# A mixture-of-experts layer on one core: where TensorE's code behind the expert loop begins within a fetch block

## The chip, the cores and the metric

The kernel runs on one core of a Trainium2 chip. The metric is the device time of one execution in microseconds (us), the median of three runs. Beside the times there is one profiled execution, whose trace holds every instruction of the engines (PE for TensorE, DVE for VectorE, ACT for ScalarE, POOL for GpSimd, SP for SyncE) and every DMA packet, among them the packets by which the engines fetch their own instructions.

## The reference

One decoder layer with 256 tokens and a model width of 2048: token mixers (attention and a gated branch), a norm, and then a mixture of 16 experts, which is where the change lies. Each token goes to two experts of one group of four.

```python
def grouped_moe(h, router_w, router_b, w_gate, w_up, w_down):
    ...
    aff = jax.nn.softmax(logits, axis=-1)
    ...
    best_group = jnp.argmax(group_score, axis=-1)
    ...
    top_val, top_idx = lax.top_k(masked, TOP_K)
    top_w = top_val / top_val.sum(-1, keepdims=True)
    combine = jnp.sum(jax.nn.one_hot(top_idx, N_EXPERTS, dtype=jnp.float32) * top_w[..., None], axis=1)
    ...
    for e in range(N_EXPERTS):
        hid = jax.nn.silu(t @ w_gate[e]) * (t @ w_up[e])
        y = y + combine[:, e:e + 1] * (hid @ w_down[e])
    return y.reshape(B, S, D)
...
    f = grouped_moe(hm, router_w, router_b, exp_w_gate[l], exp_w_up[l], exp_w_down[l])
    x = layer_norm(DEEPNORM_ALPHA * x + g2 * f, ln2_g[l], ln2_b[l])
```

Everything is float32. One expert has 2048 x 1024 weights for gate, for up and for down.

## The kernel before, in words

SP queues the weights in order as 2 MB loads into a ring of buffers in SBUF; a load waits until PE has used the buffer that it overwrites (L713). From about 778 us on, the weights of the 16 experts are streamed, and PE, DVE and ACT run through the experts in step. PE gathers an expert's tokens into slots, multiplies them with gate and up, turns the result, multiplies with down, and scatters the rows back by matmuls (`add_up`, L941, which waits for DVE).

The code of an expert depends on the number of its tokens, which is known only when the kernel runs. `CLASSES` (L43) names the cases: up to 32 tokens (`few`), up to 64 (`wide`), and then `one_extra`, `two_extra` and `all_extra` with further sets of slots. The code for `few` stands in the loop `pe_experts` itself. For every expert PE loads the count (L1665) and asks once whether it is above 32 (`ask_once`, L821). If it is, PE jumps out of the loop, to code that stands behind the whole loop and behind the kernel's last part. That code is built by `begin_and_go_on` (L830): a part `more`, which asks for the class (L835) and holds the beginning of each class (`begin`) and a jump to the body (L842); and the body of each class with the rest of the expert, a semaphore's increment (L846) and a return to the loop (`leave`, L853). The jump's target can be announced by a hint: L1219 in the `few` code for the jump of the next expert, L840 for the jump to the body, L1253 for the return.

With the tokens of this data four experts are above 32: the third of the first group (107 tokens, `two_extra`), the third and the fourth of the second group (65, `one_extra`, and 51, `wide`) and the first of the last group (90, `one_extra`). The bodies have 2173, 1293, 539 and 1293 instructions.

The loop's start is set in this way already, to slot 100 (`LOOP_SLOT`, L1657). Behind the loop stands `pe_experts_end` with the last norm's matmuls (L1673 to L1685, helper line L1280), which ends with the jump to the program's end (L279), and behind that the `more` parts and bodies of all 16 experts, four bodies each.

Of the kernel before, what the change touches and what calls it, by code (L numbers as in the profile page):

```python
# [275 lines left out]
def program(nc, x_tok_d, x_T_d, c_T_d, rel_bias_d, router_w_d, router_b_d, ada_w_d, ada_b_d, ada_bT_d, w_in_d,  # L276
            sgu_g_d, sgu_b_d, sgu_wT_d, sgu_bias_d, w_branch_d, w_out_d, ln1_g_d, ln1_b_d, ln2_g_d, ln2_b_d,
            w_up_gate_d, w_down_d, square_d, slots_d, buckets_d, out_d):
    with ExitStack() as ctx:  # L279
# [550 lines left out]
        def begin_and_go_on(eng, kind_of_engine, name, count, here, begin, body):  # L830

            with nc.body(f"{name}_more", parent=here, valid_engines=[kind_of_engine]):
                for most, kind, xs in CLASSES[:-1]:
                    above = nc.cur_bb
                    eng.br_cond(count > most, on_true=f"{name}_begin_{kind}", on_false=f"{name}_up_to_{most}")  # L835
                    nc.switch_bb(f"{name}_up_to_{most}", parent=above)
                for most, kind, xs in reversed(CLASSES):
                    if kind != CLASSES[-1][1]:
                        nc.switch_bb(f"{name}_begin_{kind}", parent=here)
                    announced = eng.mark_branch_hint_location()  # L840
                    begin(xs)
                    eng.br(f"{name}_{kind}").branch_hint(announced)  # L842
            for most, kind, xs in reversed(CLASSES):
                with nc.body(f"{name}_{kind}", parent=here, valid_engines=[kind_of_engine]):
                    announced = body(xs)
                    eng.sem_inc(extra_end[kind_of_engine], 1)  # L846
                    leave(eng, f"{name}_end", announced)

        large_announced = {}

        def leave(eng, label, announced):

            jump = eng.br(label)  # L853
            if announced is not None:
                jump.branch_hint(announced)
# [422 lines left out]
        def _(pe):  # L1278
            def mm(out, lhsT, rhs, start, stop):
                return nc.tensor.matmul(out, lhsT, rhs, start=start, stop=stop)  # L1280
# [399 lines left out]
            for a in range(TT):  # L1680
                pe.wait_ge(scale_ready, a + 1)
                for q in BY_PE[a]:
                    pe.wait_ge(centred_ready, 4 * a + q + 1)
                    mm(psum[NORM_BANKS[a][q]][:, :], row_scale[a], acc[:, a, q * 512:(q + 1) * 512], False, True)\
                      .then_inc(normed_full, 1)  # L1685
            for g, le, count, here in asked:
                begin_and_go_on(pe, mybir.EngineType.PE, f"pe{g}_{le}", count, here,
                                lambda xs: expert_pe(pe, mm, g, le, xs, BEGIN),
                                lambda xs: expert_pe(pe, mm, g, le, xs, REST))
# [297 lines left out]
        def _(dve):  # L1987
# [433 lines left out]
            def turn_of_experts(g, more):  # L2421
# [170 lines left out]
                def rest():  # L2592

                    for le, (ne, e, count, here) in enumerate(asked):
                        begin_and_go_on(dve, mybir.EngineType.DVE, f"dve{g}_{le}", count, here,
                                        lambda xs: expert_dve(ne, e, le, xs, BEGIN),
                                        lambda xs: expert_dve(ne, e, le, xs, REST))
# [101 lines left out]
```

## Time and profile before

| | |
|---|---|
| median of 3 runs | 1773.4 us |
| the runs | 1770.65 to 1774.57 us |
| span of the profiled execution | 1768.5 us |
| PE busy | 1509.3 us (85%) |
| PE weight loads busy | 1002.6 us (57%) |
| DVE busy | 589.0 us (33%) |
| DMA, mean over the span | 357 GB/s |
| granted clock of TensorE, mean | 0.932 |
| instruction packets of PE's queue | 122 packets, 2.00 MB |

The span runs from the first to the last instruction of the one execution that was profiled; the times are of other executions of the same program.
### The profile page before, as it was taken

The numbers are of one execution on the slowest core, as the hardware profiler recorded it, in microseconds if no ns is written. First come the engines' busy times: TensorE is split into PE (matmuls) and PEld (weight loads), VectorE is DVE, ScalarE is ACT, GpSimd is POOL, SyncE is SP. The second block draws the span as 40 slices with busy tenths as digits, with TensorE's granted clock in tenths as the row PEclk, the third lists the DMA queues.
The fourth block names the chain that finished last, engine by engine and source line by source line (L and its number), as shares of the span: only waits on it lengthen the run. The fifth ranks groups of instructions, "written<-read, shape, count | busy, mean of one in ns | idle before, by whom it ended". The sixth has DMA issues, their size and how long they took to land.

```text
span 1768.5 us, 27368 instructions
## 1 busy us (share of the span) xinstructions
PE 1509.3 (85%) x11924; PEld 1002.6 (57%) x11924; DVE 589.0 (33%) x1079; ACT 182.6 (10%) x442; POOL 361.6 (20%) x161
## 2 busy tenths in 40 slices
PE   7799999999999999986799966798976557898556
PEld 6578888888888878653444522433434224335222
DVE  0453657877676243431111211112020110222014
ACT  0001013101010100141100100100101001001001
POOL 0005730178677867300000000000000000000000
PEclk9899999999999999988899978898998788999888
DMA  9997896678778754549997899998999999999996
GB/s 386 424 427 218 351 393 250 250 321 370 313 310 338 285 224 174 221 171 427 426 409 282 334 427 426 425 425 347 420 427 427 425 429 426 422 411 419 428 426 248
DMA packets 51059, 630.56 MB, mean 357 GB/s; under 512 B 5775, under 2 KB 8240, under 8 KB 11848
## 3 DMA queue, kind: packets, MB, share of 16 engines
q1 hardware_dynamic: 49768, 623.15, 85.1%
q10 hardware_dynamic: 1120, 5.01, 0.7%
q8 instruction: 122, 2.00, 0.5%
q14 instruction: 49, 0.40, 0.1%
HBM read 624.47 MB, written 3.67 MB: 355 GB/s over the span
## 4 chain that ended last, share of the span: by engine, by line
PE 59%; DMA 32%; DVE 4%; issue 2%; POOL 1%; SPq 0%; DVEq 0%; ACT 0%; POOLq 0%
PE bank L1518 23%; PE bank L908 14%; DMA ring<-in_w_up_gate 9%; DMA ring<-in_w_down 9%; PE bank L1280 8%; PE bank L920 6%; DMA region_g<-in_w_up_gate 5%; DMA ring<-in_ada_w 4%; DMA region_g<-in_w_down 4%; PE bank L877 2%; PE bank L1356 2%; PE bank L932 2%; DVE ada_rows L2067 2%; DMA ring<-in_w_in 1%; POOL ring L762 1%
## 5 line engine op out<-in xcount | busy, mean ns | idle before, releaser
L762 POOL TENSOR_TENSOR ring<-ring 128x1024 f32<-128x1024 f32 x152 | 359.2, 2390 | 329.0 <-DMA ring<-in_w_in 224.0
L908 PE MATMUL bank<-ring,region_b 128*32 128x256 f32 (+1 forms) x3104 | 307.0, 478 | 122.9 <-DMA ring<-in_w_up_gate 96.9
L908 PEld LDWEIGHTS bank<-ring,region_b 128*32 128x32 f32 (+1 forms) x3104 | 129.5, 128 | 279.9 <-issue 141.7
L920 PE MATMUL bank<-ring,region_f 128*32 128x256 f32 (+1 forms) x1984 | 176.7, 451 | 60.8 <-DMA ring<-in_w_down 60.6
L1518 PE MATMUL bank<-ring,region_a 128*128 128x256 f32 x768 | 171.3, 380 | 0.5 <-ACT region_g L1863 0.5
L1518 PE MATMUL bank<-ring,region_x 128*128 128x256 f32 x768 | 170.4, 379 | 0.8 <-issue 0.7
L1518 PEld LDWEIGHTS bank<-ring,region_a 128*128 128x128 f32 x768 | 145.3, 190 | 23.0 <-issue 2.7
L920 PEld LDWEIGHTS bank<-ring,region_f 128*32 128x32 f32 (+1 forms) x1984 | 74.1, 122 | 146.9 <-issue 68.0
L1518 PEld LDWEIGHTS bank<-ring,region_x 128*128 128x128 f32 x768 | 145.3, 190 | 21.0 <-issue 1.1
L2555 DVE TENSOR_TENSOR work<-work,bank 128x128 f32<-128x128 f32 (+1 forms) x32 | 10.3, 321 | 424.8 <-ACT work L1771 424.8
L2067 DVE SCALAR_TENSOR_TENSOR bank<-ring,condT,bank 128x512 f32<-128x512 f32 x192 | 144.8, 754 | 5.8
L2513 DVE TENSOR_TENSOR region_a<-bank,region_a 128x512 f32<-128x512 f32 x96 | 59.6, 682 | 80.2 <-PE bank L932 80.1
L1280 PE MATMUL bank<-region_a,ring 128*128 128x256 f32 x384 | 84.9, 379 | 0.0
L1280 PEld LDWEIGHTS bank<-region_a,ring 128*128 128x128 f32 x384 | 72.3, 190 | 10.3 <-issue 1.0
L2067 DVE SCALAR_TENSOR_TENSOR ada_rows<-ring,condT,ada_rows 128x512 f32<-128x512 f32 x86 | 64.6, 751 | 6.7 <-DMA ring<-in_ada_w 3.9
L877 PEld LDWEIGHTS bank<-region_e,region_x 128*128 128x128 f32 x512 | 61.5, 202 | 1.8 <-DVE region_e L2417 1.8
L877 PE MATMUL bank<-region_e,region_x 128*128 128x128 f32 x512 | 61.6, 283 | 1.0 <-DVE region_e L2417 1.0
L1771 ACT ACTIVATE work<-bank 128x128 f32<-128x128 f32 (+1 forms) x32 | 9.7, 304 | 493.6 <-PE bank L908 493.6
L908 PE MATMUL bank<-region_g,region_b 128*32 128x256 f32 (+1 forms) x448 | 42.5, 456 | 17.7 <-DMA region_g<-in_w_up_gate 16.2
L908 PE MATMUL bank<-ring,region_c 128*32 128x256 f32 x896 | 51.8, 381 | 0.0
L1697 ACT ACTIVATE region_b<-bank,modcol 128x128 f32<-128x128 f32 x128 | 48.1, 456 | 30.8 <-PE bank L877 30.8
L1356 PE MATMUL bank<-region_a,ring 128*128 128x256 f32 x192 | 45.0, 391 | 1.7 <-DVE region_a L2094 0.9
(248 smaller groups left out, 1279.9 us busy)
## 6 DMA issues: line engine op xcount, KB each, us to landing
ring<-in_w_up_gate SPq DMA_DIRECT2D x111, 2048.0 KB, 29.3
ring<-in_w_down SPq DMA_DIRECT2D x56, 2048.0 KB, 21.9
ring<-in_ada_w SPq DMA_DIRECT2D x44, 2048.0 KB, 11.9
ring<-in_w_in SPq DMA_DIRECT2D x31, 2048.0 KB, 14.1
region_g<-in_w_up_gate SPq DMA_DIRECT2D x16, 2048.0 KB, 25.2
ring<-in_w_branch SPq DMA_DIRECT2D x8, 2048.0 KB, 14.4
ring<-in_w_out SPq DMA_DIRECT2D x8, 2048.0 KB, 10.3
region_g<-in_w_down SPq DMA_DIRECT2D x8, 2048.0 KB, 31.3
```

The lines of the kernel that those rows point to most:

```text
L762: ins = pool.tensor_tensor(quarter(s, *out)[:, k:k + 4, :], quarter(s, *in0)[:, k:k + 4, :], quarter(s, *in1)[:, k:k + 4, :], op)
L877: last = nc.tensor.matmul(psum[SUM_BANKS[b]][:, kk * P:(kk + 1) * P], x1[:, a, k * P:(k + 1) * P], hot[:, a, 2 * pair:2 * pair + 2, :].rea ...
L908: last = nc.tensor.matmul(bank_of(x, j)[n * c:n * c + n, 0:2 * m], tokens(x, 8 * half + k), w[:, k % 4, :, m * c:m * c + m], start=(half = ...
L920: last = nc.tensor.matmul(bank_of(x, q)[n * c:n * c + n, 0:m], hidT[x][:, k, :], w[:, k % 4, m * c:m * c + m], start=(k == 0), stop=(k == ...
L932: return nc.tensor.matmul(bank, ones_t[n * c:n * c + n, a, :], y[n * c:n * c + n, :], start=True, stop=True, tile_position=(n * c, 0))
L1280: return nc.tensor.matmul(out, lhsT, rhs, start=start, stop=stop)
L1356: last = nc.tensor.matmul(bank[:, h * T:(h + 1) * T], w[:, c * P:(c + 1) * P], xmT[:, k, :], start=k == 0 and h == 0, stop=k == KC - 1, sk ...
L1518: last = nc.tensor.matmul(bank, lhs[:, k, :], rhs[:, k, :], start=fresh and k == 0, stop=k == half - 1, skip_group_check=True)
L1697: ins = act.activation(xe[:, k, pair * P:(pair + 1) * P], psum[SUM_BANKS[b]][:, kk * P:(kk + 1) * P], ACT.Identity, scale=modcol[:, 2 * KC ...
L2067: ins = dve.scalar_tensor_tensor(out=row if k == KC - 1 else dst, in0=w[:, k, :], scalar=condT[:, k:k + 1], in1=so_far, op0=ALU.mult, op1= ...
L2513: return dve.tensor_tensor(dst, bank[:, :].rearrange("p (a n) -> p a n", a=TT), dst, ALU.add)
L2555: dve.tensor_tensor(hid[j][:, 0:m], silu_g[j][:, 0:m], psum[j][:, m:2 * m], ALU.mult)\
```

## The change

A helper `new_block` aligns PE's code to slot 0 of the next fetch block. It is called in three places: at the end of each `more` part, behind each body's return, and at the end of `pe_experts_end`, behind the norm's last matmul and ahead of the `more` parts. On the other engines it does nothing.

```diff
@@ -840,11 +840,18 @@
                     announced = eng.mark_branch_hint_location()
                     begin(xs)
                     eng.br(f"{name}_{kind}").branch_hint(announced)
+                new_block(eng, kind_of_engine)
             for most, kind, xs in reversed(CLASSES):
                 with nc.body(f"{name}_{kind}", parent=here, valid_engines=[kind_of_engine]):
                     announced = body(xs)
                     eng.sem_inc(extra_end[kind_of_engine], 1)
                     leave(eng, f"{name}_end", announced)
+                    new_block(eng, kind_of_engine)
+
+        def new_block(eng, kind_of_engine):
+
+            if kind_of_engine == mybir.EngineType.PE:
+                eng.addr_align(bass.FETCH_BLOCK_INSTRUCTIONS, offset=0, max_nops=0)
 
         large_announced = {}
 
@@ -1683,6 +1690,7 @@
                     pe.wait_ge(centred_ready, 4 * a + q + 1)
                     mm(psum[NORM_BANKS[a][q]][:, :], row_scale[a], acc[:, a, q * 512:(q + 1) * 512], False, True)\
                       .then_inc(normed_full, 1)
+            new_block(pe, mybir.EngineType.PE)
             for g, le, count, here in asked:
                 begin_and_go_on(pe, mybir.EngineType.PE, f"pe{g}_{le}", count, here,
                                 lambda xs: expert_pe(pe, mm, g, le, xs, BEGIN),
```

What stands in a row on PE at the end of `pe_experts_end` (the norm's matmuls on `region_g` and `region_a`, the jump to the end) and at the first `more` part behind it, before:

```order
L1280 MATMUL bank<-region_g,square 128x512 x6
L1280 MATMUL bank<-region_a,work 128x512 x6
L279 UNCONDITIONAL_BRANCH
L835 COMPARE_AND_BRANCH x3
L840 BRANCH_PREFETCH_HINT
L908 MATMUL bank<-ring,region_b 64x512 x8
L842 UNCONDITIONAL_BRANCH
```

The same place of the changed kernel, whose line numbers are higher by 7 or 8 here:

```order
L1287 MATMUL bank<-region_g,square 128x512 x6
L1287 MATMUL bank<-region_a,work 128x512 x6
L854 ISA
L279 UNCONDITIONAL_BRANCH
L835 COMPARE_AND_BRANCH x3
L840 BRANCH_PREFETCH_HINT
L915 MATMUL bank<-ring,region_b 64x512 x8
L842 UNCONDITIONAL_BRANCH
```

One instruction is new, the alignment (L854), between the last matmul and the jump to the program's end; what it moves is everything behind it, by the number of slots that it fills.

On PE at the end of a body, with the last scatters (L932 before, L939 after), the return and the next expert's `more` part, before:

```order
L920 MATMUL bank<-ring,region_f 64x512 x16
L932 MATMUL bank<-sgu_wT,region_d 128x512 x8
L853 UNCONDITIONAL_BRANCH
L835 COMPARE_AND_BRANCH x3
L840 BRANCH_PREFETCH_HINT
```

And in the changed kernel:

```order
L927 MATMUL bank<-ring,region_f 64x512 x16
L939 MATMUL bank<-sgu_wT,region_d 128x512 x8
L860 UNCONDITIONAL_BRANCH
L835 COMPARE_AND_BRANCH x3
L840 BRANCH_PREFETCH_HINT
```

No row comes of the calls behind a return or behind a jump to a body. The order on DVE, ACT, POOL and SP is the same.

## Rows read from the trace of the kernel before

**Rows 1.** The page's head: span, busy time of the engines, DMA in 40 slices.

```profile
span 1768.5 us, 27368 instructions
...
PE 1509.3 (85%) x11924; PEld 1002.6 (57%) x11924; DVE 589.0 (33%) x1079; ACT 182.6 (10%) x442; POOL 361.6 (20%) x161
...
DMA  9997896678778754549997899998999999999996
```

**Rows 2.** Busy time by stretch: from:to us, length, engines (instructions), PEclk, DMA share, GB/s.

```profile
960.00:980.00 20.00, 20.00 (x233) 9.45 (x234) 9.78 (x17) 0.38 (x1) 0.00 (x0) 1.00 0.58 221
...
1223.00:1231.00 8.00, 0.26 (x2) 0.29 (x4) 1.39 (x3) 0.00 (x0) 0.00 (x0) 0.69 0.81 332
1231.00:1240.00 9.00, 9.00 (x32) 2.97 (x31) 0.60 (x2) 0.00 (x0) 0.00 (x0) 0.71 0.25 83
1290.00:1300.00 10.00, 6.50 (x92) 4.21 (x87) 0.79 (x3) 0.00 (x0) 0.00 (x0) 0.83 1.02 431
1300.00:1500.00 200.00, 129.53 (x1627) 70.26 (x1620) 22.88 (x53) 18.00 (x52) 0.00 (x0) 0.84 1.01 427
1590.00:1600.00 10.00, 7.71 (x106) 4.53 (x108) 4.17 (x8) 0.00 (x0) 0.00 (x0) 1.00 0.93 381
```

**Rows 3.** PE in order of time: start, length, operation, idle before it and its releaser.

```profile
882.06 6.62 PE L908 MATMUL bank<-ring,region_b 128*64 128x512 f32 x16 [3.16 <-DVE region_a L2513]
...
984.47 3.53 PE L932 MATMUL bank<-sgu_wT,region_d 64*128 64x512 f32 x10
...
1143.65 5.35 PE L908 MATMUL bank<-ring,region_b 128*64 128x512 f32 x16 [1.57 <-DVE region_a L2513]
...
1230.74 9.79 PE L908 MATMUL bank<-ring,region_b 128*64 128x512 f32 x32 [7.89 <-issue]
...
1294.02 6.21 PE L908 MATMUL bank<-ring,region_b 128*32 128x256 f32 x80 [3.50 <-issue]
...
1513.36 5.01 PE L908 MATMUL bank<-ring,region_b 128*64 128x512 f32 x16 [5.95 <-DMA ring<-in_w_up_gate]
```

**Rows 4.** PE's jumps by line: count, ns shortest/median/longest, first and last start.

```profile
L821 PEldq COMPARE_BRANCH  x16: 75/82/6551, 786.5 to 1689.1; - x16
...
L842 PEldq COMPARE_BRANCH  x4: 232/6189/6655, 882.1 to 1513.5; - x4
...
L842 PEldq COMPARE_BRANCH  x1: 6351/6351/6351, 1143.8 to 1143.8; - x1
...
L853 PEldq COMPARE_BRANCH  x4: 324/346/431, 987.3 to 1591.7; - x4
...
L853 PEldq COMPARE_BRANCH  x1: 431/431/431, 1222.3 to 1222.3; - x1
```

**Rows 5.** The same view: loop's alignment, program's end, waits of `add_up` (two stretches).

```profile
L1657 PEldq COMPARE_BRANCH  x1: 230/230/230, 778.4 to 778.4; - x1
...
L279 PEldq COMPARE_BRANCH  x1: 3754/3754/3754, 1759.2 to 1759.2; - x1
...
L279 PEldq DRAIN  x1: 59/59/59, 1763.0 to 1763.0; - x1
...
L279 SPq DRAIN  x1: 7/7/7, 1768.3 to 1768.3; - x1
...
L941 PEldq EVENT_SEMAPHORE  x2: 51/1376/2702, 1214.4 to 1219.9; - x2
...
L941 PEldq EVENT_SEMAPHORE  x2: 51/1376/2702, 1583.8 to 1589.3; - x2
```

**Rows 6.** PE's instruction packets (count, MB, share), 1205:1222, then 1213.5:1215.

```profile
q8 instruction: 1, 0.02, 0.4%
...
q8 instruction: 1, 0.02, 4.6%
```

**Rows 7.** The same, 1583.9:1586.

```profile
q8 instruction: 1, 0.02, 3.3%
```

**Rows 8.** The same, 1142.5:1150.

```profile
q8 instruction: 2, 0.03, 2.2%
```

## The prediction

> **What bounds the kernel now.** The page comes first [rows 1]: TensorE (PE) is busy 85% of the span, and the DMA row stands at 9 in most slices behind the router, with dips. The averages don't tell what a change of code addresses is worth, so the second view is the busy time by stretch [rows 2]. The reader is to look at the DMA share beside PE's busy time. From 960 to 980 us PE is busy all the time (20.00 of 20) while the DMA share is 0.58: here PE sets the end, and its 233 matmuls and 234 weight loads run through without a gap, although they fill more than one fetch block of 256 instructions. From 1223 to 1231 PE is busy 0.26 of 8 us, and the DMA share then falls to 0.25 until 1240, since the loads wait for buffers that PE frees late. From 1590 to 1600 it is 0.93, so a delay there counts in part. From 1300 to 1500 the DMA share is 1.01 and PE is busy 129.53 of 200: a late PE costs nothing.
>
> The third view is PE's order of time at the places where it leaves the expert loop [rows 3]. Four experts have more tokens than the loop's 32 slots and take a detour: a jump to a `more` part, a jump to a body, and a return. The idle time stands there: 3.16 us ahead of 882.06, 1.57 ahead of 1143.65, 7.89 ahead of 1230.74 and 5.95 ahead of 1513.36 (put down to a weight DMA).
>
> The fourth view gives the jumps themselves [rows 4]. The question that leads to `more` (L821) is asked sixteen times: the median of 0.08 us is that of the twelve answered with no, and the longest, 6.55, ends the idle time ahead of 1230.74. The jump from the begin part to the body (L842) ran four times, 0.23 to 6.66 with a median of 6.19, and 6.35 at 1143.8. All four returns (L853) took only 0.32 to 0.43. So a jump whose target is not there costs about 6.2 to 6.7 us, and one whose target is there 0.2 to 0.4. That is the price list for everything below.
>
> **What the change does, part by part.** The difference in order holds one thing: a row behind the last matmul of the norm part, ahead of the jump to the program's end. The other calls of `new_block` stand behind unconditional jumps, and no row comes of them. So the bodies are not each put on slot 0: everything behind `pe_experts_end` is shifted as one piece. The loop is the same, instruction by instruction and slot by slot. No engine but PE is touched, and no wait, DMA or matmul is added.
>
> Step 1, the new jump over the padding. Its like is in the trace: the alignment ahead of the loop took 0.23 us (L1657) [rows 5]. If its target were absent it would cost up to 6.66 [rows 4]. It runs at 1759.2, where PE's jump to the end took 3.75 us and PE had drained at 1763.0, while SP drains at 1768.3 behind the output [rows 5]. The cover is 5.3 us, so the cost is 0, at worst 6.66 - 5.3 = 1.4. I take 0, since the padding lies right behind code that runs on in sequence.
>
> Step 2, the entries. I count positions in the built code, 256 instructions to a block. If a jump target that falls on the last 16 slots is pushed on to the next block (an assumption of the counting), the four `more` parts begin at slots 74, 66, 66, 54 before and 0, 0, 0, 0 after; the bodies at 103, 82, 176, 70 before and at 29, 16, 110, 16 after. `more` with its begin parts is at most 112 instructions up to the jump to the body, and lies within one block in both. So every jump on the way in goes from a block to another one, as before, with its hint the same number of instructions ahead: none of the long ones goes away. Their sum is 0. From below: if instructions become usable as a block's packet lands, a target 54 to 74 slots nearer to the block's start could be there earlier. One instruction packet lies wholly within 1.5 us (1213.5 to 1215) [rows 6]; 74/256 of that is 0.4 us, on seven entries (four `more` parts, three bodies in blocks of their own) not more than 2.8. The rows show no case of it, and I take 0.
>
> Step 3, the bodies. Their lengths are the same (2173, 1293, 539 and 1293 instructions), and each crosses as many block ends as before (8, 5, 2, 5). In the long body PE has no gap at such an end [rows 2], so nothing is to be gained, nor lost, inside.
>
> Step 4, the returns: here something moves. The two one_extra bodies end at slots 94 and 82 before, at slot 28 after. The block that holds the return is entered 94 or 82 instructions ahead of it before, and 28 after. That packet between 1213.5 and 1215 is the only one from 1205 to 1222 [rows 6]: it is the return's target, fetched some 8.5 us ahead of the return at 1222.3. At the other body the packet lies between 1583.9 and 1586 [rows 7] for a return at 1591.7. After the change that block is entered behind the wait of `add_up` (L941), which began at 1214.4 and took 2.70, so ended at 1217.1; the second one ran at 1219.9 [rows 5]. Counting the price of a missing target, 6.19 to 6.35 us [rows 4], from 1217.1 at the earliest gives 1223.3 to 1223.5; before, the return was through at 1222.3 + 0.43 = 1222.7. If the sequencer reaches the entry (10 of the 17 instructions between the two waits) only at about 1218.7, it is 1224.9 to 1225.1. So the return is later by 0.6 to 2.4 us. I take 1.2, nearer to the early end, since weight loads are issued ahead of their matmuls. PE sets the end there [rows 2], so it counts in full. At the other body the two waits lie at 1583.8 + 2.7 = 1586.5 and at 1589.3 [rows 5], the return at 1591.7 took some 0.35 (the median of the four) [rows 4]: the same +1.2, of which the DMA share of 0.93 [rows 2] leaves little; I take a quarter, 0.3. The long body's return goes from slot 227 to 153, and its block is still entered over ten us ahead (153 instructions with the row of ten L932 matmuls of 3.53 us among them) [rows 3]: 0. The wide body's return goes from slot 202 to 136; its hint (L1253) then runs 32 instructions behind the block's entry, and before 98. If it is dropped there, PE is 6 us late at 1287, but the DMA share is 1.02 from 1290 to 1300 [rows 2] and from 1300 to 1500 PE is busy 129.53 of 200: 0 to 2, and I take 0.
>
> A rule of the Trainium skill bears on step 4. The returns of 0.32 to 0.43 us [rows 4] are jumps far away that cost nothing. "Runtime: NRT & Kernel Launch", section "Instruction fetch mechanics", says that prefetch is purely sequential and that a taken branch whose target lies outside a window of two pages forces a fetch before execution goes on. By that each return would cost a fetch in both kernels and step 4 would be 0; these four rows speak against it, and the kernel's hints are what the rule leaves out.
>
> **The sum.** Step 1: 0; step 2: 0; step 3: 0; step 4: 1.2 + 0.3 = 1.5. The profiled execution spans 1768.5 us and the median of the runs is 4.9 above it; 1768.5 + 1.5 = 1770.0 of span, or 1773.4 + 1.5 = 1774.9 of time. A measurement of this kernel tells about 0.2% from no change, 3.5 us; the three runs lie 3.9 us apart. So the forecast is: no difference that can be measured.
>
> **Rivals.** (a) Slower by the returns. If the target is asked for only when PE has passed the last wait of `add_up`, the price counts from 1219.9: 1226.1 to 1226.3, +3.5; at the other body 1589.3 + 6.2 = 1595.5 against 1592.1, +3.4, half of it counted since so long a stop outlasts the loads under way: together +5.2, 1778.6. It decides when the packet ahead of the return starts behind 1220. For it: the hint runs long before, and its block is now entered only in the wait's shadow. Against: before, the packet came ahead of the end of these waits, by the block's entry.
>
> (b) Slower by targets at a block's end. Without the push of step 2, `more` begins at slots 253, 245, 245 and 233, and its begin part runs over the block's end after 3 to 23 instructions. That end has to be fetched in plain sequence; the row for such a stop is 3.50 us in the loop at 1290.52 (PE idle until 1294.02) [rows 3], and a full wait is 6.35. For the two hinted experts some 5 each, for the third 2 (its own stop of 7.89 holds a fetch already), for the fourth 2 beside the weights' wait: +14, 1787. The rows don't decide between the two counts; the push has the larger chance since the loop's head, too, is placed by the builder and not by the plain count.
>
> (c) Faster. On entering `more`, a packet comes besides the one that is needed: two between 1142.5 and 1150 [rows 8]. If the unneeded one is launched only from some slot on, an entry at slot 0 could come to its jump before it is launched, and the jump would cost what it does with nothing queued ahead, 3.75 [rows 5] in place of 6.19 to 6.66: -2.9 and -2.6 in full for the first two experts, -1.2 for the fourth (half of 2.4, beside the wait for weights), 1773.4 - 6.7 = 1766.7. Against: no row shows a mark inside a block, and a launch by the entry alone fits the same packets.
>
> (d) The shift isn't what the count says, or addresses don't matter: 0, 1773.4.
>
> **How the numbers follow.** The forecast has 0.73, (a) 0.10, (b) 0.07, (c) 0.07, (d) 0.03. Faster by over 0.2%: 0.07. Within 0.2%: 0.73 + 0.03 = 0.76. Slower: 0.10 + 0.07 = 0.17. The range takes in the forecast with its bounds (from below step 2 and the scatter of the runs, 1774.9 - 2.8 - 1.6 = 1770.5; from above the far ends of step 4, 2.4 + 0.6, and 2 for the wide return, 1773.4 + 5.0 = 1778.4) and with them (a), 1778.6 with 0.9 of scatter: 1770.5 to 1779.5. (b) and (c), 0.14, lie outside.
>
> **What would show it.** Right: the returns (L853) at 1222 and 1591 take 1 to 3 us in place of 0.43 and 0.35, with their packet behind 1217; the three long jumps L842 stay at 6.0 to 6.7 and L821 at 6.55 for the third expert; the new jump takes 0.2 us ahead of the jump to the end. Wrong: L842 well below 6 (then (c)), a new stop between L821 and L842 (then (b)), or a change in the loop itself, which this account excludes.

## The result and the profile after

The changed kernel takes 1783.23 us (median of 5 runs, 1781.8 to 1786.68) against 1772.45 for the kernel before in the same comparison: 1.0063 times as long (95% interval 1.0051 to 1.0076), or 10.8 us more. The forecast was 1774.9 with a range up to 1779.5, so it was wrong: the change is slower, and clearly so.

The head of the page of the changed kernel answers to [rows 1]; the busy time of each engine is the same within 3.1 us, and there is one instruction more:

```profile
span 1781.4 us, 27369 instructions
...
PE 1511.3 (85%) x11924; PEld 999.5 (56%) x11924; DVE 589.4 (33%) x1079; ACT 182.9 (10%) x442; POOL 361.3 (20%) x161
...
DMA  9997896678777664459996999997999999998996
```

PE's jumps of the changed kernel (line, count, ns shortest/median/longest, first and last start) answer to [rows 4] and [rows 5]. L860 is the return (L853 before), L854 the new jump over the padding, L948 the wait of `add_up` (L941 before):

```profile
L821 PEldq COMPARE_BRANCH  x16: 68/78/4735, 789.2 to 1701.3; - x16
...
L842 PEldq COMPARE_BRANCH  x4: 223/6354/6608, 884.4 to 1520.3; - x4
...
L860 PEldq COMPARE_BRANCH  x4: 319/2900/5927, 989.6 to 1598.9; - x4
...
L860 PEldq COMPARE_BRANCH  x1: 5372/5372/5372, 1226.5 to 1226.5; - x1
...
L860 PEldq COMPARE_BRANCH  x1: 5927/5927/5927, 1598.9 to 1598.9; - x1
...
L854 PEldq COMPARE_BRANCH  x1: 417/417/417, 1771.4 to 1771.4; - x1
...
L279 PEldq COMPARE_BRANCH  x1: 5405/5405/5405, 1771.9 to 1771.9; - x1
...
L948 PEldq EVENT_SEMAPHORE  x2: 51/1378/2704, 1218.3 to 1223.9; - x2
```

The reader is to see that the long jumps to the bodies (L842) are what they were, and that two of the four returns now cost a whole fetch: 5.37 us where it was 0.43, and 5.93 where it was 0.34. That is 4.94 + 5.59 = 10.5 us, against 10.8 measured.

That the two agree so closely is in part chance. Followed along PE's rows, the two profiled executions, whose spans differ by 12.9 us, are 2.7 us apart at the loop's first question (786.5 and 789.2), ahead of all that the change moves, and 2.3 at the first jump to a body; 4.2 apart when the first late return begins (1222.3 and 1226.5); 7.2 apart when the second one begins (1591.7 and 1598.9). So the first late return added only about 3: 4.9 less 1.8, since the question behind it (L821) took 4.74 us in place of 6.55. The second added 5.7. Of the 4.2 ahead of it, 1.8 arose between the jump to the first one_extra body and its return, 80.4 us in place of 78.6. That this comes of the slots is not shown: with the slots of before, the stretch took 78.6 to 79.3 in five profiles (before, e1, e4, e9, e10), but one and the same kernel took 80.7 in e11 and 78.8 in e12.

PE's instruction packets (count, MB, share) from 1205 to 1229 us and then from 1229 to 1231 show when the first of these two targets was asked for:

```profile
q8 instruction: 1, 0.02, 0.3%
...
q8 instruction: 1, 0.02, 3.4%
```

The first row's packet is the block that holds the return. The target's own packet lies behind 1229, while the return began at 1226.5. Before, that packet lay some 8 us ahead of the return [rows 6].

PE in order of time shows what stands behind each late return. The first answers to the row of 1230.74 in [rows 3], where the idle time was 7.89; the second to the row of the kernel before that stands last here, with 0.77:

```profile
1237.94 12.28 PE L915 MATMUL bank<-ring,region_b 128*64 128x512 f32 x46 [11.12 <-issue]
...
1605.87 3.64 PE L915 MATMUL bank<-ring,region_b 128*32 128x256 f32 x32 [6.45 <-issue]
```

```profile
1593.04 1.93 PE L908 MATMUL bank<-ring,region_b 128*32 128x256 f32 x32 [0.77 <-issue]
```

Why the time that these stops cost does not come back is seen in the busy time by stretch (the last two columns are the DMA share and GB/s). The changed kernel:

```profile
1222.00:1232.00 10.00, 4.71 (x16) 1.76 (x16) 5.66 (x9) 0.00 (x0) 0.00 (x0) 0.84 0.90 381
1232.00:1242.00 10.00, 4.06 (x10) 1.37 (x12) 0.60 (x2) 0.00 (x0) 0.00 (x0) 0.50 0.14 49
1242.00:1252.00 10.00, 10.00 (x48) 3.62 (x46) 0.00 (x0) 0.00 (x0) 0.00 (x0) 0.98 0.74 287
1596.00:1606.00 10.00, 3.44 (x16) 1.34 (x16) 5.33 (x10) 0.00 (x0) 0.00 (x0) 0.91 0.72 282
1606.00:1616.00 10.00, 10.00 (x134) 5.46 (x136) 0.12 (x1) 0.37 (x2) 0.00 (x0) 0.75 0.56 211
```

The same places of the kernel before (the stretch from 1590 to 1600 stands in [rows 2] with 0.93):

```profile
1220.00:1230.00 10.00, 2.82 (x8) 1.18 (x8) 4.16 (x7) 0.00 (x0) 0.00 (x0) 0.80 0.89 370
1230.00:1240.00 10.00, 9.26 (x32) 3.26 (x34) 0.60 (x2) 0.00 (x0) 0.00 (x0) 0.69 0.29 101
1240.00:1250.00 10.00, 10.00 (x50) 3.49 (x48) 0.42 (x1) 0.75 (x2) 0.00 (x0) 1.00 1.03 439
...
1600.00:1610.00 10.00, 10.00 (x139) 7.29 (x132) 0.29 (x1) 2.44 (x7) 0.00 (x0) 1.00 1.00 420
```

At the first place the DMA engines lose 1.0 + 8.6 + 2.6 = 12.2 us of their time after the change and 1.1 + 7.1 - 0.3 = 7.9 before: 4.3 more. At the second it is 2.8 + 4.4 = 7.2 against 0.7: 6.5 more. Together that is 10.8 us; a share of 1.03 shows that a row can be off by some 0.3 us, so this is an estimate, good to about 1 us. Between these places, and behind them until 1720 us before and 1731 after, the DMA engines are busy all the time in both kernels, so nothing wins this back. Before and then after:

```profile
1250.00:1590.00 340.00, 256.54 (x2661) 125.26 (x2657) 48.43 (x102) 29.06 (x82) 0.00 (x0) 0.89 1.01 424
1610.00:1720.00 110.00, 71.72 (x901) 36.53 (x903) 13.71 (x28) 7.49 (x22) 0.00 (x0) 0.84 1.01 427
```

```profile
1252.00:1596.00 344.00, 266.31 (x2678) 127.63 (x2674) 47.87 (x101) 29.87 (x84) 0.00 (x0) 0.87 1.00 424
1616.00:1731.00 115.00, 78.15 (x969) 40.64 (x961) 13.89 (x29) 9.31 (x27) 0.00 (x0) 0.84 1.01 427
```

### The profile page after: what moved, and what is told of

Read it like the earlier page. It is cut to its first block, busy times and chain, and to the rows that moved or that the text cites. A ratio compares the mean times of both kernels' runs of the same rounds, so it can differ in the third digit from the quotient of the medians.

```text
span 1781.4 us, 27369 instructions
## 1 busy us (share of the span) xinstructions
PE 1511.3 (85%) x11924; PEld 999.5 (56%) x11924; DVE 589.4 (33%) x1079; ACT 182.9 (10%) x442; POOL 361.3 (20%) x161
## 4 chain that ended last, share of the span: by engine, by line
PE 62%; DMA 30%; DVE 3%; issue 2%; POOL 1%; SPq 1%; DVEq 0%; ACT 0%; POOLq 0%
PE bank L1525 23%; PE bank L915 14%; DMA ring<-in_w_down 9%; DMA ring<-in_w_up_gate 9%; PE bank L1287 8%; PE bank L927 6%; DMA region_g<-in_w_up_gate 5%; PE bank L1363 4%; DMA region_g<-in_w_down 4%; PE bank L884 2%; DMA ring<-in_ada_w 2%; PE bank L939 2%; DMA ring<-in_w_in 1%; POOL ring L762 1%; PE bank L934 1%
```

## The experiments

The theories were: **A**, the hinted target is asked for when PE's sequencer enters the block that holds the return, and this entry now lies behind the wait of `add_up`; **B**, the hint is lost because it now runs in the first slots of its own block. In what follows the waits of `add_up` are counted in one_extra's instructions: the first stands 38 ahead of the return, so a return at slot s has its block entered s - 38 instructions ahead of that wait (behind it where that is negative).

**The slots of before, with the new jump (e1).**

```diff
-                eng.addr_align(bass.FETCH_BLOCK_INSTRUCTIONS, offset=0, max_nops=0)
+                eng.addr_align(bass.FETCH_BLOCK_INSTRUCTIONS, offset=77, max_nops=0)
```

> The one alignment behind the norm's last matmul is kept, but to slot 77, which gives every part behind the loop the slots that it had before the change. If the time of the changed kernel comes from the slots alone (every theory below), the returns L860 take 0.3 to 0.45 us again and the time is 1771 to 1775. If it comes from the additional jump or from anything else in the change, it stays at 1781 to 1786.

Measured: 1771.36 us, ratio 0.9995 (0.9985 to 1.0004); the returns took 0.32, 0.34, 0.35 and 0.43 us. The additional jump costs nothing; the slots are the whole cause.

**The hint moved ahead, the return kept at slot 28 (e2).** In one_extra, `mark_branch_hint_location()` is called ahead of the second half's turn (`turn(hid[1], ...)`) in place of ahead of section F.

```diff
+            if len(xs) == 1:
+                announced = pe.mark_branch_hint_location()
             pe.wait_ge(hid_ready, ne * 2 + 2)
...
-            announced = pe.mark_branch_hint_location() if base == WIDE else None
+            if not (len(xs) == 1):
+                announced = pe.mark_branch_hint_location() if base == WIDE else None
```

> The changed kernel, with one_extra's hint for its return moved 76 instructions ahead, from slot 20 of the block before the return's to slot 200 of the block before that; the return stays at slot 28 and its block is entered behind the same wait. Theory A (the return's target is asked for when its block is entered, and entering now falls into the shadow of add_up's wait): both returns still take 3 to 6 us, 1780 to 1785. Theory B (a hint that runs in the first slots of its block, while this block's successor is still to be fetched, is lost): both returns take 0.3 to 0.5 us, 1771 to 1775.

Measured: 1785.24 us, ratio 1.0060 (1.0044 to 1.0077); the two returns took 6.09 and 6.19 us. An earlier hint changes nothing, so B falls here.

**The same edit in the kernel before (e4).**

> The kernel before, with one_extra's hint moved 76 instructions ahead: to slot 10 of its block in the second group's body, and to slot 254 of the block before in the last group's. The returns stay at slots 94 and 82, whose blocks are entered ahead of the waits. Theory A: both returns 0.3 to 0.5 us, 1771 to 1775. Theory B: the second group's return takes 5 to 6 us, the last group's 0.3 to 0.5; 1776 to 1779.

Measured: 1772.07 us, ratio 0.9993 (0.9983 to 1.0003); both returns 0.34 us. A hint at slot 10 of its block is not lost. B is out.

**Slot 32 (e3).** The edit is that of e1 with `offset=32`.

> The one alignment to slot 32: the return of the second group's one_extra lies at slot 49, so its block is entered ahead of add_up's first wait, with the hint at slot 41 of the block before; the last group's return lies at slot 37, so its block is entered just behind that wait, with the hint at slot 29. Theory A: the first return takes 0.3 to 1.5 us, the second 5 to 6; about 1777. Theory B: both 5 to 6 us where slots 29 and 41 are still too early for a hint (1782), or both 0.3 to 0.5 where they are not (1772).

Measured: 1781.49 us, ratio 1.0048 (1.0032 to 1.0064); in the profiled execution the return at slot 49 took 0.43 us and that at slot 37 took 6.27. In one and the same kernel the entry ahead of the wait is served and the entry behind it is not, as A has it (e13 below narrows this). The time lies above the 1777 that were expected.

**Another body (e7).** `offset=108` puts the two_extra return on slot 12 and leaves the others far from any edge.

> The one alignment to slot 108: both one_extra returns lie at slot 143 and the wide one at 251, all entered far ahead; the two_extra return of the first group lies at slot 12, so its block is entered behind both waits of add_up. Theory A: that return takes 5 to 6.5 us in place of 0.32, the other three 0.3 to 0.5. PE sets the end there, so the time is 5 to 7 above the kernel before: 1777 to 1780. If only the one_extra bodies can lose their hint, all four take 0.3 to 0.5 and the time is 1771 to 1775.

Measured: 1777.71 us, ratio 1.0038 (1.0026 to 1.0051). The returns in order of time:

```profile
L860 PEldq COMPARE_BRANCH  x1: 5308/5308/5308, 989.4 to 989.4; - x1
...
L860 PEldq COMPARE_BRANCH  x1: 427/427/427, 1231.5 to 1231.5; - x1
...
L860 PEldq COMPARE_BRANCH  x1: 332/332/332, 1296.4 to 1296.4; - x1
...
L860 PEldq COMPARE_BRANCH  x1: 332/332/332, 1601.5 to 1601.5; - x1
```

Only the one whose block is entered behind the waits is late, and here it is another body in another group. The mechanism is not one_extra's own.

**Asking again in the return's block (e5).** The hint stands between the two parts of `add_up`, in the return's block.

```diff
-            announced = pe.mark_branch_hint_location() if base == WIDE else None
+            if len(xs) != 1:
+                announced = pe.mark_branch_hint_location() if base == WIDE else None
...
+            if len(xs) == 1:
+                announced = pe.mark_branch_hint_location()
             add_up(1)
```

> The changed kernel, with one_extra's hint moved into the return's own block, between add_up's two parts (slot 6, return at slot 28, about 2.6 us ahead of it). Theory A1 (the target is asked for on entering the block, and the answer takes 8 to 9 us): both returns still 5.4 to 6.2 us, 1781 to 1785. Theory A2 (on entering behind a wait nothing is asked at all; only the jump itself asks): the hint asks on its own, 2.6 us ahead of the jump, so both returns take 2.8 to 3.6 us, 1777 to 1780.

Measured: 1780.46 us, ratio 1.0045 (1.0028 to 1.0062); the returns took 5.69 and 5.83 us. The hint brought nothing, although it ran ahead of the last wait and 5.3 us ahead of each return. By the expectation this speaks for A1.

**More time behind the waits (e6).**

```diff
             add_up(1)
+            if len(xs) == 1 and (g, le) in ((1, 2), (3, 0)):
+                for _ in range(8):
+                    pe.value_load(counts[0:1, 0:1], min_val=0, max_val=T)
```

> The changed kernel with eight loads of a register (about 0.65 us each, some 5.2 us together) ahead of the return in two bodies, the second group's and the last group's one_extra; they change nothing that is computed. The second group's block is still entered behind add_up's first wait, but now some 10 us ahead of the return; the last group's is entered one instruction ahead of that wait. Theory A1: the second group's return 0.3 to 0.7 us. Theory A2: still 5 to 6 us. The last group's return: 0.3 to 0.5 us under either if one instruction is enough, 5 to 6 if not (A2). The time holds the filler and is no measure.

Measured: 1783.28 us with the filler in it (ratio 1.0063, 1.0041 to 1.0084). The two returns:

```profile
L860 PEldq COMPARE_BRANCH  x1: 442/442/442, 1226.5 to 1226.5; - x1
...
L860 PEldq COMPARE_BRANCH  x1: 1056/1056/1056, 1600.5 to 1600.5; - x1
```

PE's instruction packets from 1215 us to 1226.5, where the first of the returns begins:

```profile
q8 instruction: 1, 0.02, 0.6%
```

With about 5 us more behind the waits the target is asked for ahead of the jump, so the sequencer doesn't need the jump itself to ask: the strict form of A2 falls. It fits A1 for the first return (0.44), although its block is entered behind the first wait. The second, entered one instruction ahead of the first wait, still lost 0.7 us, although its block had been entered some 13 us ahead (that wait began at 1587.3).

**What a late PE costs (e9, e10).** Sixteen register loads on PE in the kernel before, at two places, without any late return.

```diff
             add_up(1)
+            if base == WIDE and not xs and (g, le) == (1, 3):
+                for _ in range(16):
+                    pe.value_load(counts[0:1, 0:1], min_val=0, max_val=T)
```

(e10 has `len(xs) == 1 and (g, le) == (3, 0)` as the condition.)

> The kernel before, with sixteen loads of a register (0.65 us each, 10.4 us together; nothing computed from them) on PE ahead of the wide body's return, at about 1287 us. Theory C (a late PE costs nothing as long as loads are under way, and the DMA time that is lost once they run out is never regained): the DMA share stays near 1.0 from 1290 on, since PE has slack there until 1500; 1772 to 1776. If every delay of PE in the expert loop counts in full: 1783.

> The kernel before, with the same sixteen loads ahead of the return of the last group's one_extra body, at about 1592 us. Theory C: some 3 us of the 10.4 lie in the slack, then the DMA queue runs dry and the rest is lost for good: +6 to +9, 1779 to 1782. If only a quarter counts, as the prediction took it: +2.6, about 1775.

Measured: e9 1778.81 us, ratio 1.0032 (1.0020 to 1.0044), 5.7 us more; e10 1784.89 us, ratio 1.0069 (1.0043 to 1.0094), 12.2 us more. The busy time by stretch of e9 and then of e10:

```profile
1290.00:1300.00 10.00, 0.22 (x4) 0.23 (x8) 1.78 (x4) 0.00 (x0) 0.00 (x0) 0.58 0.88 375
1300.00:1310.00 10.00, 10.00 (x134) 5.45 (x130) 0.03 (x1) 0.28 (x1) 0.00 (x0) 0.73 0.57 213
```

```profile
1590.00:1600.00 10.00, 5.03 (x18) 1.86 (x16) 5.66 (x9) 0.00 (x0) 0.00 (x0) 0.98 0.89 355
1600.00:1610.00 10.00, 3.78 (x40) 2.10 (x44) 0.60 (x2) 0.00 (x0) 0.00 (x0) 0.51 0.01 2
1610.00:1620.00 10.00, 10.00 (x171) 6.10 (x164) 0.29 (x1) 0.94 (x3) 0.00 (x0) 1.00 0.91 365
```

The DMA time that is lost, 1.2 + 4.3 = 5.5 us and 1.1 + 9.9 + 0.9 - 0.7 = 11.2 us (0.7 is what the kernel before loses there), gives the price of both within 1 us, although the profiled execution of e9 was the fastest of its ten (1774.73). Of a delay of 10.4 us at the wide body about half is covered by loads under way, where I expected nearly all; at the last group none of it is, where I expected 3 us.

**Nearer to the wait (e11).** `offset=38`.

> The one alignment to slot 38: the blocks of both one_extra returns (slots 55 and 43) are entered ahead of add_up's first wait, the last group's only five instructions ahead of it. If being ahead of the wait is enough: both returns 0.3 to 0.5 us and 1771 to 1775. If five instructions are too few: the last group's return 4 to 6.3 us and 1778 to 1782.

Measured: 1781.1 us, ratio 1.0049 (1.0033 to 1.0064); the return at slot 55 took 5.39 us and that at slot 43 took 0.43. Neither expectation came true: the one entered 17 instructions ahead of the wait was late, the one entered 5 ahead was not. So A in its simple form doesn't hold near the wait.

**The same kernels again (e12 to e14) and slot 52 (e15).** e12, e13 and e14 are the kernels of e11 and e3 and the changed kernel, unaltered; e15 has `offset=52`.

> A second look at the alignment to slot 38, where the return at slot 55 took 5.39 us and that at slot 43 took 0.43. If the position decides: 5.4 and 0.4 again. If it is a race near the wait: at least one of the two may come out the other way.

> A second look at the alignment to slot 32, where the return at slot 49 took 0.43 us and that at slot 37 took 6.27. If the position decides: the same. If it is a race: the return at slot 49 may be late now; the one at slot 37, entered behind the wait, stays late (5 to 6.3).

> A second look at the changed kernel itself (slot 0, both returns at slot 28, entered behind the wait). Under either reading both returns are late again, 5 to 6.3 us: here it is no race.

> The alignment to slot 52: the returns lie at slots 69 and 57, entered 31 and 19 instructions ahead of add_up's first wait. If the race reaches only some 20 instructions ahead of the wait, slot 69 takes 0.3 to 0.5 us and slot 57 may take either; if it reaches further, either may be late.

Measured, one profile each: the two returns took 6.35 and 5.80 us in e12, 5.92 and 5.71 in e13, 6.03 and 5.57 in e14, 0.34 and 5.95 in e15; the times were 1782.02, 1781.17, 1783.57 and 1779.12 us, beside 1771.1 for the kernel before. The one_extra returns of the kernels without a filler, with the bodies in their order and the hint in its place or earlier, in us:

| return's slot | block entered ahead of the first wait, instructions | returns |
|---|---|---|
| 28 | -10 | 5.37, 5.93 (after), 6.03, 5.57 (e14), 6.09, 6.19 (e2) |
| 37 | -1 | 6.27 (e3), 5.71 (e13) |
| 43 | 5 | 0.43 (e11), 5.80 (e12) |
| 49 | 11 | 0.43 (e3), 5.92 (e13) |
| 55 | 17 | 5.39 (e11), 6.35 (e12) |
| 57 | 19 | 5.95 (e15) |
| 69 | 31 | 0.34 (e15) |
| 82 | 44 | 0.34 (before), 0.43 (e1), 0.34 (e4) |
| 94 | 56 | 0.43 (before), 0.34 (e1), 0.34 (e4) |
| 143 | 105 | 0.43, 0.33 (e7) |

The same code came out once served and once late at slots 43 and 49, so near the wait it is a race that falls out by execution. Behind the wait all eight returns were late. From 31 instructions ahead on, all nine were served.

**Another order of the bodies (e8).** A test of the price list of the jumps, and the only candidate for a gain.

```diff
-            for most, kind, xs in reversed(CLASSES):
+            for most, kind, xs in (CLASSES[2], CLASSES[3], CLASSES[1], CLASSES[0]):
                 with nc.body(f"{name}_{kind}", parent=here, valid_engines=[kind_of_engine]):
```

> The kernel before (no alignment behind the loop) with the bodies in another order: one_extra right behind the begin parts, then wide, two_extra, all_extra. The jump from begin to body lies within one block for the two one_extra experts and leads far away for the wide one. By the price list of the jumps: L842 of about 0.2 us for the second group's third expert (6.35 before) and for the last group's (6.03), 6 to 6.7 for the wide one (0.23). PE is then 6 us earlier and 6 later within the second group, and 6 earlier in the last group, where 3 us of slack lie already: 1769 to 1775.

Measured: 1772.07 us, ratio 0.9986 (0.9972 to 1.0000). The jumps to one_extra took 0.22 and 0.21 us, as the price list has it; that to the wide body took 4.36, less than the 6 to 6.7 expected, at a DMA share of 0.06 while it ran. But neither the gain nor the loss reaches PE's work. The first matmul of the body behind the first of these jumps, which began at 1143.8 before and at 1148.7 in e8; before and then in e8:

```profile
1150.39 1.92 PE L981 MATMUL bank<-region_x,region_e 128*32 128x512 f32 x16 [1.38 <-DVE region_e L2443]
```

```profile
1155.16 1.92 PE L981 MATMUL bank<-region_x,region_e 128*32 128x512 f32 x16 [1.29 <-DVE region_e L2443]
```

With the jump of 6.35 us it starts 6.6 us behind the jump's start. With that of 0.22 it starts 6.5 us behind it, since now it has to wait for DVE. From the jump's start to that of the body's return, the three bodies took 78.6, 56.4 and 78.2 us before and 78.5, 56.1 and 78.8 in e8. So the long jumps to the bodies are covered, and no version beats the kernel before by more than the measurement can tell.

## Why the prediction was wrong, step by step

**What bounds the kernel** was right in that PE sets the end at the detours and the DMA engines do between them. But "a late PE costs nothing" from 1300 to 1500 went too far: the delay of 10.4 us in e9 cost 5.7. The **price list** was right in kind: in the expert loop, a jump whose target is neither there nor under way takes 4.4 to 7.3 us over all these runs (below 5.3 only at DMA shares of 0.24 and less), one whose target is there 0.2 to 0.4. It lists the time of the jump, though, which e8 shows to cost PE next to nothing at L842.

**What the change does** was right: one alignment is built, everything behind it shifts as one piece, and no other engine changes. e1 shows that nothing but the slots matters.

**Step 1** was right in size: the new jump took 0.42 us (0.23 was expected) at 1771.4, and PE had drained 4 us ahead of the end of the span. The jump to the end behind it took 5.41 in place of 3.75, which the prediction did not foresee; it ended 4 us ahead of the end of the span too.

**Step 2** was right: the three long L842 stay at 6.29 to 6.61 us. One term was not foreseen: the unhinted question of the second group's fourth expert took 4.74 in place of 6.55, and this gave 1.8 us back. It fits that its fetch met DMA engines that had run idle: of the seven profiles with a late first return, six have 4.4 to 5.3 us here, at DMA shares of 0.09 to 0.24 while the question ran, and e5 has 6.03 at 0.30; the ten with a first return served in time have 6.4 to 7.3 (0.83 before). Rivals (b) and (c) didn't happen: no new stop between L821 and L842, no cheaper L842, and by e8 a cheaper L842 would have gained nothing that shows.

**Step 3** stays open: the body ahead of the first late return took 1.8 us more in this profile, and no run ties that to the slots or clears them of it.

**Step 4** failed, in two terms. The place was right, and so was the sign: the two one_extra returns, because their block is entered behind `add_up`'s wait; the other two unchanged (0.32 and 0.43). The first wrong term is the price. I counted the 6.2 us of a fetch from the entry of the block, and so came to 0.6 to 2.4 us for each return. The packets came 2.9 and 3.6 us behind the returns' own starts, so each fetch ran as if nobody had asked ahead, and each return lost 4.9 and 5.6. Rival (a) held the same mechanism with a later start, behind the last wait, and still came to only +3.5 and +3.4. Its sign, a packet that starts behind 1220, came, but later than (a) had it: behind the start of the return, not ahead of it. The second wrong term is the weight. At the last group I let a quarter count (a half in the rival), since the DMA share was 0.93 there. The stop let the loads run out, 6.5 us of DMA time were lost, and since the DMA engines set the pace to the end, none of it came back. With the prices measured and both counted in full, the sum is 10.5 us, or 8.7 with the 1.8 that came back at L821; behind the start of the first late return the two profiled executions differ by just these 8.7.

**The range** failed with it: its upper end took the 5.2 of rival (a). A row for the full price stood in [rows 4] already, 6.19 to 6.66 for a jump that isn't served, and the honest far end of a return that may be asked for too late was that price at both places, less the 0.4 of a served return: +11.6 to +12.5.

A rule of the Trainium skill ("Runtime: NRT & Kernel Launch", section "Instruction fetch mechanics") says that a taken branch out of the two-page window forces a fetch before execution goes on. In the prediction the four cheap returns spoke against it; two of these four show it now (5.37 and 5.93). In these runs a hint suspends the rule only where its fetch is sent in time.

**What is shown and what stays open.** Shown: the slots alone are the cause (e1); not the hint's place (e2, e4); a return whose block is entered behind `add_up`'s wait is late in every profile with nothing put in behind that wait, in two kinds of body (the changed kernel, e2, e3, e7, e13, e14); near the wait it is a race (e11 to e13). Not shown is why the request isn't sent on entry in those cases: neither the passing of the waits nor a hint between them (e5) brought it ahead of the jump, while a stretch of register loads did (e6). That the sequencer sends it only in a stretch without waits fits these runs, but no run tells it from other readings.

## What to carry to other kernels

Code placement counted here through the distance between the start of a jump's fetch block and the waits ahead of the jump: where a hinted jump leads far away, let its block be entered well ahead of any semaphore wait (31 instructions ahead of the first wait were enough here, 19 were not), and look at the slots of the jumps rather than at those of the bodies' beginnings. Before pricing a long jump, see whether PE has other work or another wait behind it, as at L842. When a stop on PE is priced in a stretch that streams weights, add up the DMA time that it loses and count it in full wherever the DMA share is 1.0 up to the end. And if the argument says that something comes too late, its far end is the full price of not having it.

## What was not expected of the hardware

A branch hint that ran 20 us ahead of its jump, as that of the changed kernel did (L1260, last at 1579.1, for a jump at 1598.9), didn't help when the block of the jump was entered behind a wait. The same kernel can have a hinted jump of 0.43 us in one execution and of 5.80 or 5.92 in the next (slots 43 and 49). And the same unhinted jump took 4.74 us with the DMA engines nearly idle (share 0.22 while it ran), against 6.55 while they were streaming (0.83).
